# Ten raw chunks overwritten by their low parts, and six high parts, in place of rings of 8, 4 and 4

## The reference, cut to what matters

```python
h = jnp.matmul(_rmsnorm(x, norm_g).astype(x.dtype), w_in).astype(jnp.float32)   # w_in_ab, w_in_c: 2048 x 8192
...                                                                             # attention, gate
return x + jnp.matmul(y.astype(x.dtype), w_out)                                 # w_out_ab, w_out_c: 2048 x 2048
# second block: rmsnorm, modulation, then x @ w_in_2 (context and latent tokens), mixing, @ w_out_2,
# rmsnorm, @ peer_wq_2, choice of experts, weighted sum over rows of peer_u_2 and peer_v_2, final rmsnorm
```

## Time and profile before

| | |
|---|---|
| median of 3 runs | 3197.98 us (3191.51 to 3199.49) |
| span of the profiled execution | 3186.2 us (the page gives no other time of it) |
| PE busy | 2993.9 us, 94% |
| DVE busy | 2380.2 us, 75% |
| ACT busy | 1888.2 us, 59% |
| DMA moved | 792.95 MB |
| weight GEMMs end | at about 1765 us |

### The profile page before, as it was taken

How to read it: one execution, slowest core, us unless ns; L and a number is a source line. 1 busy time by engine, 2 the same in 40 slices (tenths; PEclk the granted TensorE clock), 3 DMA queues, 4 the chain that set the end, 5 groups by cost and what they waited for, 6 DMA issues and landing times.

```text
span 3186.2 us, 40248 instructions
## 1 busy us (share of the span) xinstructions
PE 2993.9 (94%) x12354; PEld 2183.9 (69%) x12354; DVE 2380.2 (75%) x4369; ACT 1888.2 (59%) x4178; POOL 306.5 (10%) x372
## 2 busy tenths in 40 slices
PE   7999999999999999988889599899999999999998
PEld 6777878888887877776677233333333888888886
DVE  6787776888767657875867899999999555555556
ACT  5555545555556765444455587788887555555555
POOL 1000000000000000000000233333332000000000
PEclk9999999999999999997999655555555999999999
DMA  7666666777767557970555699999999655555554
GB/s 256 207 206 200 219 225 216 257 241 238 234 239 237 177 166 237 342 285 7 200 192 166 250 413 413 381 406 413 413 421 383 227 195 186 195 186 195 186 196 146
DMA packets 214208, 792.95 MB, mean 249 GB/s; under 512 B 17410, under 2 KB 18130, under 8 KB 151458
## 3 DMA queue, kind: packets, MB, share of 16 engines
q1 hardware_dynamic: 159040, 408.99, 38.8%
q0 software_dynamic: 51344, 370.53, 29.8%
q10 hardware_dynamic: 3668, 11.53, 1.0%
HBM read 783.64 MB, written 7.34 MB: 248 GB/s over the span
## 4 chain that ended last, share of the span: by engine, by line
PE 60%; DVE 22%; DMA 10%; ACT 4%; issue 2%; DVEq 2%; ACTq 1%; SPq 0%; POOLq 0%
PE bank L545 11%; PE bank L547 11%; PE bank L546 11%; DVE u_ring L2621 8%; PE bank L2797 7%; PE bank L2799 7%; PE bank L2798 7%; DMA u_ring<-in_peer_u,idx 5%; DVE u_more L2621 4%; DVE acc L600 3%; DVE w_lo L536 3%; DMA u_more<-in_peer_u,idx 2%; DMA raw<-in_w_in 2%; ACT w_hi L532 1%; DMA raw<-in_w_out 1%
## 5 line engine op out<-in xcount | busy, mean ns | idle before, releaser
L532 ACT ACTIVATE w_hi<-raw 128x512 fp32r<-128x512 f32 x1008 | 622.2, 629 | 649.7 <-PE bank L547 577.7
L536 DVE TENSOR_TENSOR w_lo<-raw,w_hi 128x512 fp32r<-128x512 f32 x1008 | 667.5, 692 | 326.6 <-ACT w_hi L532 323.0
L545 PE MATMUL bank<-w_hi,xt_hi 128*128 128x512 f32 x1632 | 659.8, 404 | 40.5 <-DVE w_lo L536 39.9
L547 PE MATMUL bank<-w_hi,xt_lo 128*128 128x512 f32 x1632 | 638.6, 391 | 0.0
L546 PE MATMUL bank<-w_lo,xt_hi 128*128 128x512 f32 x1632 | 638.5, 391 | 0.0
L2551 PE MATMUL bank<-row_ring,one_row 96*128 96x512 bf16 x1024 | 527.2, 619 | 56.6 <-DVE act_in L2621 26.5
L2720 DVE TENSOR_TENSOR w_lo<-v_raw,w_hi 128x512 fp32r<-128x512 f32 x496 | 343.4, 693 | 282.3 <-ACT w_hi L2693 282.2
L2693 ACT ACTIVATE w_hi<-v_raw 128x512 fp32r<-128x512 f32 x496 | 313.2, 632 | 317.3 <-PE bank L2799 317.3
L2621 DVE CUSTOM_DVE_ANT_0 u_ring<-u_ring,bank 128x1024 f32<-128x1024 f32 x344 | 405.7, 1217 | 28.6 <-DMA u_ring<-in_peer_u,idx 16.2
L545 PEld LDWEIGHTS bank<-w_hi,xt_hi 128*128 128x128 f32 x1632 | 307.8, 189 | 126.9 <-DVE w_lo L536 53.9
L2797 PE MATMUL bank<-w_hi,vw_hi 128*128 128x512 f32 x992 | 392.1, 395 | 2.7 <-DVE w_lo L2720 2.7
(11 more groups left out here) (453 smaller groups left out, 3504.1 us busy)
## 6 DMA issues: line engine op xcount, KB each, us to landing
v_raw<-in_peer_v SPq DMA_DIRECT2D x128, 1024.0 KB, 4.8
ada_ring<-in_ada_w POOLq DMA_DIRECT2D x96, 1024.0 KB, 6.0
raw<-in_w_in_ab SPq DMA_DIRECT2D x128, 512.0 KB, 4.2
raw<-in_w_in_c SPq DMA_DIRECT2D x128, 512.0 KB, 4.6
raw<-in_w_in SPq DMA_DIRECT2D x120, 512.0 KB, 4.5
raw<-in_w_out_ab SPq DMA_DIRECT2D x32, 512.0 KB, 4.3
raw<-in_w_out_c SPq DMA_DIRECT2D x32, 512.0 KB, 5.7
raw<-in_w_out SPq DMA_DIRECT2D x32, 512.0 KB, 6.9
```

The costliest lines, as they stand in the source:

```text
L532: act.activation(w_hi[:, s % WS, :], raw[:, q % RAW, s % KC, :], ACT.Copy).then_inc(hi_ready, 1)
L536: dve.tensor_tensor(w_lo[:, s % WS, :], raw[:, s // KC % RAW, s % KC, :], w_hi[:, s % WS, :].bitcast(F32), ALU.subtract).then_inc(raw_used, 1)
L545: pe.matmul(o, a_hi, b_hi, start=kk == 0, stop=False, skip_group_check=True)
L547: last = pe.matmul(o, a_lo, b_hi, start=False, stop=kk == K - 1, skip_group_check=True)
```

## The change

The raw ring has RAW = 5 load buffers, ten chunks: four where it was and the fifth in the first 4 KB a partition of the old `w_hi`. The low part is written over the raw chunk (`raw_lo` is the same memory, named as the matmul's type), so there is no ring of low parts. The high parts have a ring of their own, HI = 6. Together they take the memory of the three rings before. A load buffer is now given back by the multiply of its second chunk: `load_sp` waits on `chunk_multiplied`. The first five loads wait for nothing. Ring positions go by the number of the load over the whole program. The fifth load of `mix_out` waits also for `ml_taken` 16, as its buffer lies in `v_one`. SP's loops are written out. Semaphores and helpers that are no longer used go.

```diff
-RAW = 4
+RAW = 5
 WS = 4
+HI = 6
@@
-        raw = at("raw", [P, RAW, KC, N], RAW_AT)
+        raw_at = [RAW_AT + 4096 * i for i in range(RAW - 1)] + [WS_AT]
+        raw = [at(f"raw{i}", [P, KC, N], o) for i, o in enumerate(raw_at)]
+        raw_lo = [at(f"raw_lo{i}", [P, KC, N], o, F32R) for i, o in enumerate(raw_at)]
+        hi = at("hi", [P, HI, N], WS_AT + 4096, F32R)
         w_hi = at("w_hi", [P, WS, N], WS_AT, F32R)
         w_lo = at("w_lo", [P, WS, N], WS_AT + 8192, F32R)
@@
+        def load_sp(sp, d, src):
+
+            if d >= RAW:
+                sp.wait_ge(chunk_multiplied, PRE + KC * (d - RAW + 1))
+            if d == plan["mix_out"]["c0"] + RAW - 1:
+                sp.wait_ge(ml_taken, 16)
+            sp.dma_start(raw[d % RAW][:, :, :], src).then_inc(w_landed[d % RAW], 16)
+
         def stream_sp(sp, g, order=range(Q)):
             w = weights[g["name"]].rearrange("(q k p) n -> q p k n", k=KC, p=P)
-
-            def tile(n, dt):
+            for n in range(g["n"]):
+                at_ = n * N + g.get("from", 0)
                 for q in range(Q):
-                    c = g["c0"] + Q * n + q
-                    sp.wait_ge(raw_used, KC * (c + 1))
-                    sp.dma_start(raw[:, q % RAW, :, :], w[order[q]][:, :, dt(n)]).then_inc(w_landed[q % RAW], 16)
-
-            with sp.Fori(0, g["n"]) as n:
-                tile(n, lambda n: bass.ds(n * N + g.get("from", 0), N))
+                    load_sp(sp, g["c0"] + Q * n + q, w[order[q]][:, :, at_:at_ + N])
@@
         def split_hi_act(act, g, s):
 
-            q = s // KC
+            c = g["c0"] * KC + s
+            d = c // KC
             if s % KC == 0:
-                act.wait_ge(w_landed[q % RAW], 16 * (g["c0"] // RAW + q // RAW + 1))
-            act.wait_ge(chunk_multiplied, PRE + g["c0"] * KC + s - WS + 1)
-            act.activation(w_hi[:, s % WS, :], raw[:, q % RAW, s % KC, :], ACT.Copy).then_inc(hi_ready, 1)
+                act.wait_ge(w_landed[d % RAW], 16 * (d // RAW + 1))
+            if c >= HI:
+                act.wait_ge(chunk_multiplied, PRE + c - HI + 1)
+            act.activation(hi[:, c % HI, :], raw[d % RAW][:, c % KC, :], ACT.Copy).then_inc(hi_ready, 1)
 
         def split_lo_dve(dve, g, s):
-            dve.wait_ge(hi_ready, PRE + g["c0"] * KC + s + 1)
-            dve.tensor_tensor(w_lo[:, s % WS, :], raw[:, s // KC % RAW, s % KC, :],
-                              w_hi[:, s % WS, :].bitcast(F32), ALU.subtract).then_inc(raw_used, 1)
+            c = g["c0"] * KC + s
+            d = c // KC
+            dve.wait_ge(hi_ready, PRE + c + 1)
+            dve.tensor_tensor(raw_lo[d % RAW][:, c % KC, :], raw[d % RAW][:, c % KC, :],
+                              hi[:, c % HI, :].bitcast(F32), ALU.subtract).then_inc(lo_split, 1)
 
         def multiply_pe(pe, g, s, n, kk, stationary):
-            pe.wait_ge(raw_used, RAW * KC + g["c0"] * KC + s + 1)
+            c = g["c0"] * KC + s
+            pe.wait_ge(lo_split, c + 1)
             for t in range(T):
                 o = bank[:, 2 * (n % 2) + t, :]
                 a_hi, a_lo = stationary(kk, t)
-                b_hi, b_lo = w_hi[:, s % WS, :], w_lo[:, s % WS, :]
+                b_hi, b_lo = hi[:, c % HI, :], raw_lo[c // KC % RAW][:, c % KC, :]
...
         def layer_sp(sp, L):
...
-                    sp.wait_ge(raw_used, KC * (c + 1))
-                    sp.dma_start(raw[:, q % RAW, :, :], w[q][:, :, at_:at_ + N]).then_inc(w_landed[q % RAW], 16)
+                    load_sp(sp, c, w[q][:, :, at_:at_ + N])
...
-                sp.wait_ge(raw_used, KC * (g["c0"] + i + 1))
-                sp.dma_start(raw[:, i % RAW, :, :], w[(kk // KC + first) % Q][:, :, n * N:(n + 1) * N]).then_inc(w_landed[i % RAW], 16)
+                load_sp(sp, g["c0"] + i, w[(kk // KC + first) % Q][:, :, n * N:(n + 1) * N])
...
         def dve_program(dve):
-            dve.sem_inc(raw_used, RAW * KC)
```

More of the change, by code:

```diff
@@ L281, in bass_hybrid_stack_kernel @@
         out_stored = sem("out_stored")
-        passed, passed_pool = sem("passed"), sem("passed_pool")
-        raw_used = sem("raw_used")
+        passed = sem("passed")
+        lo_split = sem("lo_split")
         hi_ready = sem("hi_ready")
@@ L300, in bass_hybrid_stack_kernel @@
         (silu_done, acc_summed, row_taken, gates_multiplied, ml_a, ml_row, ml_exp, conv_turned, convolved, conv_silu, conv_scaled,
          upd_weighed, upd_multiplied, upd_taken, ml_weighted, ml_scored, ml_taken, ml_mixed, ml_exponent, ml_exped, ml_scaled,
-         mix_ready, mix_multiplied, mix_scaled, mix_gelu, mix_square, out_root, out_square, full_ready, part_copied, part_rest, part_low,
+         mix_ready, mix_multiplied, mix_scaled, mix_gelu, mix_square, out_root, out_square, part_copied, part_rest, part_low,
@@ L303, in bass_hybrid_stack_kernel @@
          back_turned, hf_stored, pq_copied, pq_turned, keys_copied, keys_kept, keys_scored, gate_shifted, gate_exped, chosen, chosen_turned,
-         rings_free, half_spread, halves_read, placed, one_hot, weights_taken, indices_copied, values_high, values_split, values_multiplied, vw_high, vw_low, gelued, wg_ready, idx_ready, mix_squared, mix_varied, mix_rooted, z_weighed, y_turned, y_high, y_low, row_summed, rows_cleared, bias_row_landed, row_multiplied, x_scaled, mod_ready, gates_added, decays_spread, coefs_taken, k_turned, cols_taken, y_ready, last_added, last_squared, last_root, last_rooted, out_scaled, sgu_landed, gates_copied, gates_turned, u_gated, pool_taken, ml_stated, sgu_w_landed, windows_landed, mlstm_g_landed) = (sem(n) for n in names.split())
+         rings_free, half_spread, halves_read, placed, one_hot, weights_taken, values_high, values_split, values_multiplied, vw_high, vw_low, wg_ready, idx_ready, mix_squared, mix_varied, mix_rooted, z_weighed, y_turned, y_high, y_low, row_summed, rows_cleared, bias_row_landed, row_multiplied, x_scaled, mod_ready, gates_added, decays_spread, coefs_taken, k_turned, cols_taken, y_ready, last_added, last_squared, last_root, last_rooted, out_scaled, sgu_landed, gates_copied, gates_turned, u_gated, pool_taken, ml_stated, sgu_w_landed, windows_landed, mlstm_g_landed) = (sem(n) for n in names.split())
@@ L366, in take_h @@
             last.then_inc(evacuated, 1)
[L368 to L416, removed]
@@ L2837, in act_program @@
         def act_program(act):
-            for s_ in (hi_ready, act_step, hi_written, qk_copied, exped, p_copied, gelued, weights_taken, values_high, vw_high):
+            for s_ in (hi_ready, act_step, hi_written, qk_copied, exped, p_copied, weights_taken, values_high, vw_high):
                 act.sem_inc(s_, PRE)
```

4 lines of the change are left out of this document (2 added, 2 removed).

## The result

The changed kernel takes 3142.8 us (median of 5 runs, 3137.7 to 3157.1) against 3191.5 us (3181.7 to 3199.5) for the kernel before in the same comparison: ratio 0.9876, 95% interval 0.9859 to 0.9892. That is about 40 us less by the ratio (34 to 45 us by its interval). Forecast were 18 us less and a range down to 3161 us. The direction was right; the size was off by a factor of more than two, and the time lies outside the range.

A forecast was written before the change was run, and what follows sets the result against it. TensorE was busy 94% of a 3186.2 us span, so only its idle time could be won. Terms of -7, -3.5, -3, -3, -2.5 and +1 us made -18 us, from 3197.98 to 3180 us; range 3161 to 3203 us.

The forecast's parts named there:

- The 60:300 stretch: 60 to 300 us, in the weight GEMMs: TensorE idle 14.1 us, 10.1 us of it waits on low parts.
- That is the most that a deeper split can give: Whole kernel: TensorE's 41 waits on low parts, 42.2 us together, were taken as the ceiling of the gain.
- The first rival: Attention steps: the lead stays at 4 or 5 and TensorE waits for these steps instead; about -5 us, 3193 us; chance 0.23.
- The third rival: All waits on low parts go, 36 us, with some attention waits behind them; 3162 us; chance 0.12.
- The base: Whole kernel: median 3197.98 us, 11.8 us over the profiled span, that part taken as unchanged.
- -7: 60 to 300 us: extra room of 2.5 us takes most of the 10.1 us of waits, less two; -7 us.
- -3.5: Before 60 and 970 to 1300 us: half of 6.8 us of waits goes; -3.5 us.
- +1 for 500:970: 500 to 970 us, no wait before: modulations meeting landings of up to 7.5 us cost 1 us.
- -2.5: 1300 to 1410 us: of 5.8 us of waits, with landings of 7.6 and up to 11.6 us, 2.5 us go.
- the second rival: Loads come too late wherever a modulation meets a slow landing; +15.5 us, 3213 us; chance 0.11.
- the cap at the tile end: Tile ends: ScalarE takes a finished tile at slot 4 of the next, so its lead there is 4 whatever the rings hold.
- The cap by the landing: Slow landings limit VectorE's room: 4.8 us at a 4.6 us landing, 1.8 at 7.6; loads too late from 7.05 us.

The follow-up runs named there:

- e1: The changed kernel with four high parts in place of six, still five load buffers; ratio 0.9999 to the kernel before.
- e2: The changed kernel with five high parts in place of six, still five load buffers; ratio 0.9924 to the kernel before.
- e6: The kernel before with each modulation after the first of a row cut to its first 64 columns; ratio 0.9872 to the kernel before.
- e7: The changed kernel with each modulation after the first of a row cut to its first 64 columns; ratio 0.9808 to the kernel before.
- e9: The changed kernel with attention steps of ScalarE and VectorE one slot later (LEAD = 6, not 5); ratio 0.9926 to the kernel before.
- e8: The changed kernel with finished tiles taken out of PSUM at slot 6 of the next tile, not slot 4; ratio 0.9879 to the kernel before.
- e10: The changed kernel with four load buffers in place of five and six high parts, 4 KB unused; ratio 1.0126 to the kernel before.
- e3: The changed kernel with three load buffers, five high parts and five separate low parts, loads released by the low part; ratio 1.0042 to the kernel before.
- e4: The changed kernel with four load buffers in place of five and eight high parts in place of six; ratio 1.0129 to the kernel before.

## Why the prediction was wrong

The mechanism was right: bursts of VectorE against the lead of the split, with the loads as what speaks against it (e1, e2, e6, e7). The 60:300 stretch came out as said, only more so: waits on low parts of 1.6 us against some 3 forecast, 500:970 full, SP waiting for matmuls (1382.8 us, all its weight loads), ScalarE waiting for landings more often, the 5.8 us at the start of mixing kept, SP's loops worth nothing. A low part written in place takes 0.68 us in the median, as before (0.69). The waits on low parts in total fell to 27.1 us; 24 were forecast.

**The step that failed** is the first one: "That is the most that a deeper split can give", said of the 42.2 us of waits on low parts. The sum was taken over one class of waits. Within that class it was nearly right: -18 us forecast, -15.1 us measured. But ScalarE and VectorE work in program order, so a split that waits less for TensorE also brings the attention steps behind it sooner. The waits on attention, residual and context inputs (12.0 us) went with the others, 6.8 us came back by the clock and some 7.4 us were gained in starts whose lateness no row shows; the sum put all three at nothing. With them the gain is larger than the 42.2 us that were called the most. The first rival had the sign of the attention waits wrong: I thought that TensorE would then wait for the attention steps instead. The third rival named them, at 0.12, but its 36 us are the waits on low parts alone. e1 and e9 show both sides: with four high parts these waits are all back, and one slot later in the order brings others (e9).

**The base** was off as well. I took 11.8 us between span and median as something that lies around the span. The profiled execution of the changed kernel has 3157.1 us for a span of 3155.3 us, so it is 1.8 us; the other 10 us were the spread of the runs, and the median of 17 later runs of the kernel before is 3185.5 us. That made the forecast 10 us too high in absolute terms. Without it the range would have reached down to 3151 us, and 3142.8 us would still lie outside.

**The terms.** Weight GEMMs of layer ab (first output matmul 420.7 to 403.8 us): -16.9 us, where -7 and a part of -3.5 were forecast. To the first context matmul (1030.5 to 1000.5): another -13.1, where +1 for 500:970 and a part of the -3.5 stood. This is the largest miss: TensorE's only wait on a low part there is the one of 2.1 us at the context GEMM's start, before and after; what went are 5.1 us of waits on attention, residuals and context, and the 6.8 us of the clock. From there to the end of the latent stage (1413.3 to 1372.4): another -10.9, where -2.5 and the rest of the -3.5 stood. The mixing and query GEMMs together: -4.5, forecast -6. In mixing I gave -3 and the waits fell by 1.6 us (13.0 to 11.4); ScalarE waited 30.1 us there for landings, 23.5 before, at a DMA share of 0.73, so it wasn't the DMA engines' time that ran out. In the query GEMM -3 against 0.9 (6.4 to 5.5).

One reading was wrong without changing the forecast: the 29 in 500 to 970 us are GpSimd's instructions, the loads of blocks; VectorE adds up 42 times there (L600), so by its own rule the second rival's price for that stretch was 19 us, not 13.

**The lead, step by step.** Of the cap at the tile end, for which the sum was lowered, no cost shows in e8 (0.9879 against 0.9876). That the lead is rebuilt before a burst comes would explain it; the lead itself was not read. The cap by the landing is real, but its threshold was one buffer away: with five buffers loads landed in a median 4.0 us from 505 to 880 us and TensorE never waited; with four the second rival came true at +35 us.

**The memory rate.** At the saturated stretch the changed kernel's loads land a little sooner, median 6.9 us in 1250 to 1370 us against 7.6, and the waits on low parts there fell from 5.8 us to 3.2. The landings, the waits, and the stretch by engine (the last number is GB/s, 363 before):

```profile
DMA to landing us min/median/max: 5.3/6.9/10.0
...
PE bank L496 <- DVE raw_lo L486: 3.2, 7, 0.7
...
1260.00:1370.00 110.00, 106.81 (x465) 85.26 (x464) 91.30 (x100) 50.72 (x89) 10.05 (x19) 1.00 1.00 373
```

So the term (-2.5) came about. The Trainium skill (DMA: Bandwidth & Descriptors, "Where 436 GB/s comes from") binds loads from HBM at about 358 GB/s a core. The trace differs: 373 GB/s in this stretch, as the expert stage's 414 GB/s had said.

## What to carry to other kernels

The waits on one hand-over are not the ceiling of what a deeper ring gives: when the engines that fill the ring work in program order, the ring's lead is also the lead of every other step on them, and with the waits half-rate pieces of the clock may go. These don't follow the idle time one for one: up to the end of the latent stage they sum to 23.9 us before and 10.2 us after, but to 17.1 us in e10, which is idle longer than before. Sum all waits of the bound engine in the stages that the ring serves, and test with the old depth in the new code. Look for memory that one value needs only after another is dead, as raw chunk and low part here: that bought the fifth load buffer and the two high parts, and the two other divisions of the same 32 KB a partition (e3, e4) were slower than the start.

## What the runs showed of the hardware

The value stage runs at one of two paces, in the same code. From the first to the last start of its matmuls (the last of them stand on other lines than those above) it took 704 to 706 us in eleven of thirteen profiles, and 718 us in those of the changed kernel and of e1. In 2600 to 3000 us, before and after:

```profile
2600.00:3000.00 400.00, 400.00 (x1749) 328.60 (x1748) 233.54 (x437) 213.56 (x438) 0.00 (x0) 1.00 0.56 191
```

```profile
2600.00:3000.00 400.00, 400.00 (x1716) 323.97 (x1716) 229.21 (x430) 209.18 (x428) 0.00 (x0) 1.00 0.55 187
```

TensorE is full and at 2.4 GHz in both, and does 2% fewer matmuls in the second; each start lies 0.233 us after the last one in place of 0.229. The cause was not looked for. The runs of the kernel before spread from 3176 to 3202 us; whether this pace makes part of that is not shown, as only one execution of each kernel was profiled.

A low part of 0.69 us lasts over 3 us where GpSimd's product of `h` and `subln` runs beside it (two of them take 3.90 us beside one of 2.42 us in the lines above). This happens twice in the kernel, at 64.7 and 167.7 us before and at 62.9 and 159.2 us after; all other low parts take at most 0.70 us. The new rings don't take it away; they only cover it. That the two are slow because of each other is read from their times; no run moves one of them.
